# A decoder step with mixture of experts: the routing's marking, ranks, weights and tables, and the order of the work around them

## The chip, the cores and the metric

The kernel runs on one core of one Trainium2 chip. The metric is the device time of one launch in microseconds (us); the kernel before has a median of 1256.03 us over 3 runs (1255.35 to 1258.71).

## The reference

One decoder layer over 576 tokens (512 of a prompt, 64 of eight sampled sequences), width 1024: attention and a gated convolution side by side, a layer norm, and then a feed-forward part. Its routing is what the change is about:

```
scores = sigmoid(x2 @ w_router)                       # 64 experts in 8 groups of 8
biased = scores + router_bias
grp_score = sum(top_k(biased by group, 2))            # keep the 4 best groups
eidx = top_k(where(in a kept group, biased, -inf), 6) # 6 experts of each token
gw = scores[eidx]; gw = gw / sum(gw) * 2.5
y = shared_expert(x2) + sum_j gw_j * expert[eidx_j](x2)
ple = sigmoid(h @ w_ple_gate) * (p @ w_ple_proj)      # added before the last norm
```

Each of the 64 experts has three weight matrices of 1 MB. All are read from HBM, whatever the routing says.

## The kernel before, in words

Tokens lie in NT = 5 tiles of 128 (the last has 64). Each engine has its own program, written out by hand; semaphores alone order the engines, and each engine and each DMA queue does its work strictly in the order written. After the first norm this happens:

- TensorE computes router logits, then the shared expert's gate and up products (`shared_half(m, k, cs)`: half m of the columns, k = 0 gate, 1 up; 6 matmuls for each of 8 chunks c). These accumulate in PSUM tensor `proj` for m = 0 and `att` for m = 1, two banks each for gate and up.
- VectorE picks the experts (lines 1900 to 1950): `max` gives the best eight values of a group or token, `max_index` their places; from these it builds one-hot rows `hot` (30 = 5 tiles x 6 choices, 64 wide) and their sum `sel`. It signals `sel_ready`.
- TensorE turns `sel` into the rank of each token at its expert by small bf16 matmuls into `proj` banks 0 and 1 (L1395, L1398). VectorE's `shared_act(0)` must have read these banks first (`hs_ready`). VectorE copies the ranks out (`rank_read`), computes the number of passes of each pair of experts, its running sum in five doubling steps (L2005, L2006), and a code of column and slot for each choice; `pick(dst, per_expert)` reads a value for each of the 30 choices by multiplying with `hot` and summing (L1964, L1967).
- Table m = 0..9: VectorE builds the pieces for three choices in one of two buffers (L2048 to L2055, `tb_ready`), TensorE multiplies them into one bank (`table_products`, L1407, `tb_used`). `weights_of(t)` on VectorE computes the gate weights of one tile of tokens before every second table. When all ten are summed, VectorE reads the bank out and signals `routed`.
- Between tables TensorE works on 20 gate units: unit u = 5 j + t is column block j (of 4) and token tile t of `h @ w_ple_gate` (L1423, 24 matmuls). N_AHEAD = 3 units stand ahead of table 0, one behind each table, the rest of blocks 0 to 2 behind those. The last block's units (15 to 19) run split in `last_block(True)`, the first transposes of gathered rows (`turn(0)`), and `last_block(False)`.
- A unit goes on through ScalarE (`gate_sigmoid(u)`, L999) and GpSimd (`ple_product(u)`). Unit u on TensorE waits for the sigmoid of unit u - 2. Each column block is loaded as float32 by SyncE (`load_gate(j)`, L587), copied by ScalarE (`gate_hi(j)`, L973), and its low part computed by GpSimd in four instructions (`gate_lo(j)`, L713). Blocks 0 to 3 use two slots, 1, 0, 1, 0. On ScalarE `gate_hi(2)` stands behind the sigmoid of unit 5 and `gate_hi(3)` behind that of unit 11, ahead of that of unit 12. GpSimd does `gate_lo(3)` behind `ple_product(11)`, and then the first gather of rows, which waits for `routed`.
- Expert weights stream through a ring of three buffers, each for a pair of experts, six parts of 1 MB (`load_part`, L595). Pair 0 is loaded when the shared products are done (`su_ready` 2). The first half of pair 1's buffer is where the routing's tables lie, its second half where gate products `ppo` and the shared activations `hs_f` lie. So parts 0 to 2 of pair 1 wait for `routed`, the others for `ppo_added` (VectorE has added units 0 to 9) and `hs_hd` (ScalarE has copied `hs_f` away, behind the sigmoid of unit 14). Pair 2's parts wait for `tb_used` 11 (the end of `last_block(True)`), for all 20 units, and for `res_done`. From pair 3 on each buffer's reload waits for the compute of the pair three before, which runs at TensorE's lines 1493 and 1512.

Of the kernel before, what the change touches and what calls it, by code (L numbers as in the profile page):

```python
# [16 lines left out]
P = 128  # L17
# [38 lines left out]
N_AHEAD = 3  # L56
# [64 lines left out]
def decoder_step(nc, x_prompt, x_sample, p_prompt, p_sample, win_k, win_v, conv_state, w_in, sinks,  # L121
# [4 lines left out]
    with ctx:  # L126
        base0 = (nc.sbuf_base + 31) // 32 * 32

        def at(name, shape, dt, off):
            return nc.alloc_sbuf_tensor_at(name, shape, dt, offset=base0 + off)  # L130
# [141 lines left out]
        hs_f = at("hs_f", [P, 2, T], F32, o_w1 + 38912)  # L272
# [21 lines left out]
        wpick = at("wpick", [P, TOPK, NE], F32, o_w1 + 43520)  # L294
# [18 lines left out]
        ghot = rsm("ghot", [P, NT, TOPG, NGRP], F32)  # L313
# [3 lines left out]
        gidx = rsm("gidx", [P, NT, 8], U32)  # L317
        gidx_f = rsm("gidx_f", [P, NT, TOPG], F32)
# [17 lines left out]
        cums = [rsm(f"cums{i}", [P, NPE], F32) for i in range(2)]  # L336
# [5 lines left out]
        hot_a = at("hot_a", [P, NT, TOPK // 2, NE], BF16, o_w1 + 4096)  # L342
        hot_b = at("hot_b", [P, NT, NE], BF16, o_w1 + 4096 + 2 * NT * TOPK // 2 * NE)
# [148 lines left out]
        def _(sp):  # L492
# [565 lines left out]
        def _(pe):  # L1058
# [329 lines left out]
            shared_half(1, 0, range(KC))  # L1388
            shared_half(1, 1, range(2))

            pe.wait_ge(sel_ready, 1)
            pe.wait_ge(hs_ready, 1)
            for t in range(NT):
                for s in range(t + 1):
                    nc.tensor.matmul(proj[:, 0, t * NE:(t + 1) * NE], (ones_b if s < t else tri_b)[:, :], sel[:, s, :],  # L1395
                                     start=(s == 0), stop=(s == t))
            for s in range(NT):
                last = nc.tensor.matmul(proj[:, 1, 0:NE], ones_b[:, :], sel[:, s, :], start=(s == 0), stop=(s == NT - 1))  # L1398
            last.then_inc(rank_ready, 1)
            shared_half(1, 1, range(2, KC)).then_inc(su_ready, 1)  # L1400
# [188 lines left out]
        def _(dve):  # L1589
# [307 lines left out]
            nc.vector.memset(scores[NS:P, NT - 1, :], 0.0)  # L1897
            dve.wait_ge(sc_ready, 1)
# [13 lines left out]
            for t in range(NT):  # L1912
                nc.vector.max_index(gidx[:, t, :], gbest[:, t, :], gsum[:, t, :])
            dve.drain()

            nc.vector.tensor_copy(gidx_f[:, :, :], gidx[:, :, 0:TOPG])
            dve.drain()
            for t in range(NT):
                nc.vector.tensor_tensor(ghot[:, t, :, :], iota64[:, 0:NGRP].unsqueeze(1).to_broadcast([P, TOPG, NGRP]),
                                        gidx_f[:, t, :].unsqueeze(2).to_broadcast([P, TOPG, NGRP]), ALU.is_equal)  # L1920
            dve.drain()
            nc.vector.reduce_sum(gmask[:, :, :], ghot[:, :, :, :].rearrange("p t i g -> p t g i"), AX.X)
            dve.drain()
            nc.vector.tensor_scalar(gmask[:, :, :], gmask[:, :, :], BIG, -BIG, ALU.mult, ALU.add)
# [8 lines left out]
            dve.drain()  # L1933
            for t in range(NT):
                nc.vector.max_index(eidx[:, t, :], ebest[:, t, :], biased[:, t, :])
# [8 lines left out]
            dve.drain()  # L1944
            hot5 = hot[:, :, :].rearrange("p (t j) e -> p t j e", t=NT)
            nc.vector.tensor_tensor(hot_a[:, :, :, :], hot5[:, :, 0:TOPK // 2, :], hot5[:, :, TOPK // 2:TOPK, :], ALU.add)
            dve.drain()
            nc.vector.tensor_tensor(hot_b[:, :, :], hot_a[:, :, 0, :], hot_a[:, :, 1, :], ALU.add)
            dve.drain()
            nc.vector.tensor_tensor(sel[:, :, :], hot_b[:, :, :], hot_a[:, :, 2, :], ALU.add).then_inc(sel_ready, 1)  # L1950
# [19 lines left out]
            def weights_of(t):  # L1970

                js = slice(t * TOPK, (t + 1) * TOPK)
                total = ssum[:, t:t + 1]
                nc.vector.tensor_tensor(wpick[:, :, :], hot[:, js, :], scores[:, t, :].unsqueeze(1).to_broadcast([P, TOPK, NE]),
                                        ALU.mult)
                dve.drain()
                nc.vector.reduce_sum(wj[:, js], wpick[:, :, :], AX.X)
                dve.drain()
                nc.vector.reduce_sum(total, wj[:, js], AX.X)
                dve.drain()  # L1980
                if t == NT - 1:
                    nc.vector.memset(ssum[NS:P, t:t + 1], 1.0)
                    dve.drain()
                nc.vector.reciprocal(total, total)
                dve.drain()
                nc.vector.tensor_scalar(wj[:, js], wj[:, js], total, ROUTED_SCALE, ALU.mult, ALU.mult)
                dve.drain()

            shared_act(0)
            dve.wait_ge(rank_ready, 1)  # L1990
            nc.vector.tensor_copy(base64[:, :], proj[:, 1, 0:NE:2])
            dve.drain()
            nc.vector.tensor_tensor(nmax[:, :], base64[:, :], proj[:, 1, 1:NE:2], ALU.max)
            dve.drain()
            nc.vector.tensor_scalar(npass_i[:, :], nmax[:, :], SLOT - 1.0, None, ALU.add)
            nc.vector.tensor_copy(rank_i[:, :, :].rearrange("p t e -> p (t e)"), proj[:, 0, 0:NT * NE]).then_inc(rank_read, 1)
            dve.drain()
            nc.vector.tensor_scalar(npass_i[:, :], npass_i[:, :], 6, None, ALU.arith_shift_right)
# [3 lines left out]
            cur = npass_f  # L2002
            for s in range(5):
                nxt = cums[s % 2]
                nc.vector.tensor_copy(nxt[:, 0:1 << s], cur[:, 0:1 << s])  # L2005
                nc.vector.tensor_tensor(nxt[:, 1 << s:], cur[:, 1 << s:], cur[:, 0:NPE - (1 << s)], ALU.add)  # L2006
                dve.drain()
                cur = nxt

            nc.vector.tensor_tensor(base64[:, :], cur[:, :], npass_f[:, :], ALU.subtract)  # L2010

# [24 lines left out]
            nc.vector.tensor_copy(slot_j[:, :], code_j[:, :].bitcast(I32))  # L2036
            dve.drain()
# [208 lines left out]
```

## Time and profile before

| | |
|---|---|
| median of 3 runs | 1256.03 us |
| the profiled execution | 1255.99 us |
| its span | 1254.2 us |
| TensorE matmul busy | 1219.1 us (97%) |
| VectorE / ScalarE / GpSimd busy | 512.2 / 314.7 / 159.3 us |
| DMA | 307.31 MB, mean 245 GB/s |

The span runs from the first to the last recorded instruction; 1.8 us of the execution lie around it. In 40 slices of 31.4 us each the page shows the DMA engines mostly at two to three tenths until about slice 20 (the end of the routing), and at nine tenths from slice 22 on to the end, at about 420 GB/s: there the expert weights stream. The granted clock is at full speed in all slices.

### The profile page before, as it was taken

To read this page: it belongs to the slowest core of one execution; us is meant where nothing else is said; L and a number is where in the kernel's file an instruction comes from. 1 tells how busy PE (TensorE), PEld (TensorE's weight loads), DVE (VectorE), ACT (ScalarE), POOL (GpSimd) and SP (SyncE) were. 2 spreads that over 40 slices of the span, in tenths; PEclk is the share of its full clock that TensorE was granted. 3 is DMA by queue.
4 is the path that set the end of the run, shared out by engine and by line. 5 is a ranking of instruction groups with operands and counts; after the bars stand their busy time and mean duration, and the time that the engine had idled before them with its cause. 6 is when DMAs were issued, how large, how long until landed. Compare 5 with 4: busy or idle time off the path is not lost.

```text
span 1254.2 us, 23439 instructions
## 1 busy us (share of the span) xinstructions
PE 1219.1 (97%) x8816; PEld 982.2 (78%) x8817; DVE 512.2 (41%) x1125; ACT 314.7 (25%) x574; POOL 159.3 (13%) x227
## 2 busy tenths in 40 slices
PE   8999989999999999999899999999999999999987
PEld 8999979999999999998899665556555566666643
DVE  4666783432444324566885112121222221111137
ACT  4364553222212222316012111111111111111121
POOL 0200000000000000004235211111121121212100
PEclk9999999999999999999999999999999999999999
DMA  8222223223232232615428999999999999999987
GB/s 265 80 60 68 68 52 68 68 70 99 68 100 69 77 110 67 213 23 208 175 94 330 420 419 420 420 420 419 420 422 418 420 422 418 419 423 420 421 352 297
DMA packets 98656, 307.31 MB, mean 245 GB/s; under 512 B 11244, under 2 KB 62404, under 8 KB 72840
## 3 DMA queue, kind: packets, MB, share of 16 engines
q1 hardware_dynamic: 85332, 275.20, 56.6%
q0 software_dynamic: 12304, 28.60, 5.9%
q10 hardware_dynamic: 948, 2.50, 0.5%
q8 instruction: 52, 0.85, 0.3%
q14 instruction: 20, 0.16, 0.0%
HBM read 294.45 MB, written 26.94 MB: 256 GB/s over the span
## 4 chain that ended last, share of the span: by engine, by line
PE 56%; DMA 37%; DVE 5%; issue 1%; DVEq 1%; SPq 0%; ACT 0%; ACTq 0%; POOLq 0%
PE proj L1072 32%; DMA w_exp<-in_w_e_down_dram 28%; DMA w_exp<-in_w_e_up_dram 7%; PE proj L1282 4%; PE proj L1423 3%; PE att L1493 3%; PE proj L1512 2%; PE att L1204 1%; PE att L1166 1%; PE att L1291 1%; PE proj L1106 1%; DMA fold<-expert_rows 1%; PE proj L1377 1%; PE proj L1407 1%; PE att L1217 1%
## 5 line engine op out<-in xcount | busy, mean ns | idle before, releaser
L1493 PE MATMUL att<-w_exp,xt 128*64 128x256 f32 x2560 | 286.2, 380 | 1.9 <-DMA w_exp<-in_w_e_up_dram 1.9
L1493 PEld LDWEIGHTS att<-w_exp,xt 128*64 128x64 f32 x2560 | 207.7, 137 | 89.0 <-issue 26.1
L1072 PE MATMUL proj<-h_hi,w_hi 128*128 128x288 f32 x768 | 167.9, 300 | 0.3 <-DVE w_lo L474 0.3
L1072 PE MATMUL proj<-h_hi,w_lo 128*128 128x288 f32 x768 | 164.0, 295 | 0.0
L1072 PE MATMUL proj<-h_lo,w_hi 128*128 128x288 f32 x768 | 163.9, 295 | 0.0
L1512 PE MATMUL proj<-w_exp,ht_e 128*64 128x512 f32 x640 | 146.2, 597 | 9.1 <-issue 5.6
L1072 PEld LDWEIGHTS proj<-h_hi,w_hi 128*128 128x128 f32 x768 | 122.3, 189 | 6.1 <-issue 4.6
L1072 PEld LDWEIGHTS proj<-h_lo,w_hi 128*128 128x128 f32 x768 | 123.6, 188 | 0.0
L1072 PEld LDWEIGHTS proj<-h_hi,w_lo 128*128 128x128 f32 x768 | 123.4, 188 | 0.0
L474 DVE TENSOR_TENSOR w_lo<-w_raw,w_hi 128x2048 fp32r<-128x2048 f32 x33 | 75.6, 2291 | 92.1 <-ACT w_hi L464 87.7
L1512 PEld LDWEIGHTS proj<-w_exp,ht_e 128*64 128x64 f32 x640 | 50.5, 136 | 77.1 <-issue 74.3
L2126 DVE TENSOR_SCALAR ysb<-proj,tabw 128x512 f32 x40 | 30.0, 751 | 139.1 <-PE proj L1512 139.1
L464 ACT ACTIVATE w_hi<-w_raw 128x2048 fp32r<-128x2048 f32 x33 | 63.0, 1910 | 84.5 <-PE proj L1072 73.9
L2117 DVE TENSOR_TENSOR sg<-sg,att 128x256 f32<-128x256 f32 x40 | 16.9, 422 | 117.1 <-ACT sg L1025 117.1
L1032 ACT ACTIVATE ysb<-proj,tabw 128x512 f32 x40 | 27.5, 687 | 140.5 <-PE proj L1512 140.5
L2121 DVE TENSOR_TENSOR h_e<-sg,att 128x256 f32<-128x256 f32 x40 | 16.9, 421 | 111.4 <-PE att L1493 111.4
L693 POOL DMA_DIRECT2D out_dram<-cn_tok x1 | 0.5, 502 | 474.9 <-ACT cn_tok L938 474.9
L1027 ACT ACTIVATE ht_e<-att 128x256 f32<-128x256 f32 x40 | 15.3, 383 | 170.9 <-PE att L1499 170.9
L768 POOL DMA_INDIRECT expert_rows<-ysb,sidx_col x39 | 39.5, 1012 | 131.8 <-DVE ysb L2126 131.8
L1433 PEld LDWEIGHTS proj<-ident,xg 128*128 128x128 f32 x328 | 43.3, 195 | 15.9 <-issue 13.9
L1072 PE MATMUL proj<-mix_hi,w_hi 128*128 128x288 f32 x256 | 54.8, 296 | 0.0
L1072 PE MATMUL proj<-mix_hi,w_lo 128*128 128x288 f32 x256 | 54.8, 296 | 0.0
(392 smaller groups left out, 1864.0 us busy)
## 6 DMA issues: line engine op xcount, KB each, us to landing
w_exp<-in_w_e_gate_dram SPq DMA_DIRECT2D x64, 1024.0 KB
w_exp<-in_w_e_up_dram SPq DMA_DIRECT2D x64, 1024.0 KB
w_exp<-in_w_e_down_dram SPq DMA_DIRECT2D x64, 1024.0 KB
w_raw<-in_w_in_dram SPq DMA_DIRECT2D x21, 1024.0 KB
part<-expert_rows SPq DMA_DIRECT2D x8, 1536.0 KB, 20.4
w_raw<-in_w_in_dram SPq DMA_DIRECT2D x8, 512.0 KB
w_raw<-in_w_attn_out_dram SPq DMA_DIRECT2D x8, 512.0 KB
w_raw<-in_w_conv_out_dram SPq DMA_DIRECT2D x4, 1024.0 KB
```

Of the source, the lines that this page charges most:

```text
L464: nc.scalar.activation(w_hi[:, g.par, :], w_raw[:, g.par, :], ACT.Copy).then_inc(hi_done, 1)
L474: nc.vector.tensor_tensor(w_lo[:, g.par, :], w_raw[:, g.par, :], w_hi[:, g.par, :].bitcast(F32), ALU.subtract).then_inc(w_ready, 1)
L768: pool.indirect_dma_start(out=rows_d[:, :], out_offset=bass.IndirectOffsetOnAxis(ap=sidx_col[i][:, 0:1], axis=0), in_=ysb[:, i, :], in_off ...
L1032: nc.scalar.activation(ysb[:, bass.ds(side_of, 1), 0:512].rearrange("p o n -> p (o n)"), proj[:, 2, :], ACT.Copy, scale=tabw[:, bass.ds(k, ...
L1072: last = nc.tensor.matmul(proj[:, 2 * i + a, 0:HALF], lhs, x[:, c, a * HALF:(a + 1) * HALF], start=(c == 0 and n == 0), stop=(c == KC - 1 ...
L1282: last = nc.tensor.matmul(out, x, v, start=(c == 0 and n == 0), stop=(c == KC - 1 and n == last_term))
L1423: last = nc.tensor.matmul(gate_bank(u)[0:w, :], x[:, c, t * P:t * P + w], v[:, c, :], start=(c == 0 and n == 0), stop=(c == KC - 1 and n = ...
L1433: last = nc.tensor.transpose(proj[:, half, c * P:(c + 1) * P], xg[:, :, half * 4 + c], ident[:, :])
L1493: last = nc.tensor.matmul(att[e * SLOT:(e + 1) * SLOT, m, 0:FF], xt[:, c, e * SLOT:(e + 1) * SLOT], weights[e][:, c, :], start=(c == 0), s ...
L1512: last = nc.tensor.matmul(proj[e * SLOT:(e + 1) * SLOT, 2 + half, :], ht_e[:, c, e * SLOT:(e + 1) * SLOT], down[e][:, c, half * 512:(half ...
L2117: nc.vector.tensor_tensor(sg[:, :], sg[:, :], att[:, 0, 0:FF], ALU.mult)
L2126: nc.vector.tensor_scalar(ysb[:, bass.ds(side_of, 1), 512:D].rearrange("p o n -> p (o n)"), proj[:, 3, :], tabw[:, bass.ds(k, 1)], None, A ...
```

## The change

Routing: groups and experts that are not in the top are no longer found through indices. `gbest`'s last four values are overwritten, `match_replace` marks the kept group scores with BIG, and a mask is made by comparing; likewise `ebest` and `replaced` give `sel`, and `sel_ready` comes before `max_index` and `hot`. The three additions that made `sel` are gone. Ranks go to bank 2 of `att`, ahead of most of `shared_half(1, 0)`; `shared_half(1, 1)`, which uses that bank, waits for `rank_read`. VectorE reads ranks ahead of `shared_act(0)`. One `tensor_tensor_scan` replaces the doubling steps; the code of column and slot takes fewer passes. The weights of all tiles are computed at once, before table 0. `shared_act(1)` stands before table 4 instead of table 2. TensorE does four units ahead of the tables, and then units behind tables 1, 3, 5, 7, 8 and 9. SyncE loads parts 0 to 2 of pair 1 ahead of gate block 3, and part 4 with part 3.

```
-N_AHEAD = 3
+N_AHEAD = 4
+UNIT_AFTER = (1, 3, 5, 7, 8, 9)
-        hs_f = at("hs_f", [P, 2, T], F32, o_w1 + 38912)
+        hs_f = at("hs_f", [P, 2, T], F32, o_w1 + 49152 - 2 * 4 * T)
+        def rank_out(t):
+            return att[:, 2, t * NE:(t + 1) * NE]
@@ SyncE
             load_gate(2)
+            sp.wait_ge(routed, 1)
+            load_parts(1, 1, range(3))
             sp.wait_ge(u_ready, 2 * NT)
             load_gate(3)
-            sp.wait_ge(routed, 1)
-            load_parts(1, 1, range(3))
             sp.wait_ge(ppo_added, 1)
-            load_parts(1, 1, range(3, 4))
+            load_parts(1, 1, range(3, 5))
             sp.wait_ge(hs_hd, 1)
-            load_parts(1, 1, range(4, 6))
+            load_parts(1, 1, range(5, 6))
@@ TensorE
-            shared_half(1, 0, range(KC))
-            shared_half(1, 1, range(2))
-
+            shared_half(1, 0, range(2))
             pe.wait_ge(sel_ready, 1)
-            pe.wait_ge(hs_ready, 1)
...
             last.then_inc(rank_ready, 1)
-            shared_half(1, 1, range(2, KC)).then_inc(su_ready, 1)
+            shared_half(1, 0, range(2, KC))
+            pe.wait_ge(rank_read, 1)
+            shared_half(1, 1, range(KC)).then_inc(su_ready, 1)
+            pe.wait_ge(hs_ready, 1)
             for u in range(N_AHEAD):
                 gate_unit(u)
-            pe.wait_ge(rank_read, 1)
             for m in range(NTK // TPAIR):
                 table_products(m)
-                gate_unit(N_AHEAD + m)
-            for u in range(N_AHEAD + NTK // TPAIR, 3 * NT):
+                if m in UNIT_AFTER:
+                    gate_unit(N_AHEAD + UNIT_AFTER.index(m))
+            for u in range(N_AHEAD + len(UNIT_AFTER), 3 * NT):
                 gate_unit(u)
@@ VectorE (max_index, gidx_f, ghot and the sum over ghot are gone)
+            nc.vector.memset(gbest[:, :, TOPG:8], 4 * BIG)
...
+                nc.vector.match_replace(gmask[:, t, :], gbest[:, t, :], gsum[:, t, :], BIG)
+            nc.vector.tensor_scalar(gmask[:, :, :], gmask[:, :, :], BIG, -BIG, ALU.not_equal, ALU.mult)
...
+            nc.vector.memset(ebest[:, :, TOPK:8], 4 * BIG)
...
+                nc.vector.match_replace(replaced[:, t, :], ebest[:, t, :], biased[:, t, :], BIG)
+            nc.vector.memset(replaced[NS:P, NT - 1, :], 0.0)
+            nc.vector.tensor_scalar(sel[:, :, :], replaced[:, :, :], BIG, None, ALU.is_equal).then_inc(sel_ready, 1)
...
-            nc.vector.tensor_tensor(hot_a[:, :, :, :], hot5[:, :, 0:TOPK // 2, :], hot5[:, :, TOPK // 2:TOPK, :], ALU.add)
-            nc.vector.tensor_tensor(hot_b[:, :, :], hot_a[:, :, 0, :], hot_a[:, :, 1, :], ALU.add)
-            nc.vector.tensor_tensor(sel[:, :, :], hot_b[:, :, :], hot_a[:, :, 2, :], ALU.add).then_inc(sel_ready, 1)
...
+            nc.vector.tensor_tensor_scan(cums[:, :], npass_f[:, :], no_steps[:, :], 0.0, ALU.add, ALU.add)
+            nc.vector.tensor_tensor(base64[:, :], cur[:, :], npass_f[:, :], ALU.subtract)
+            nc.vector.scalar_tensor_tensor(slot_map[:, :, :], col_i, float(P), slot_map[:, :, :].bitcast(I32), ALU.mult, ALU.add)
             for t in range(NT):
+                nc.vector.scalar_tensor_tensor(col_map[:, t, :].rearrange("p (q e) -> p q e", e=2),
+                                               base64[:, :].unsqueeze(2).to_broadcast([P, NPE, 2]), float(P),
+                                               slot_map[:, t, :].rearrange("p (q e) -> p q e", e=2), ALU.mult, ALU.add)
...
+            pick(wj[:, :], scores)
+            wj3 = wj[:, :].rearrange("p (t j) -> p t j", t=NT)
+            nc.vector.reduce_sum(ssum[:, :], wj3, AX.X)
+            nc.vector.memset(ssum[NS:P, NT - 1:NT], 1.0)
+            nc.vector.reciprocal(ssum[:, :], ssum[:, :])
+            nc.vector.scalar_tensor_tensor(wj3, wj3, ROUTED_SCALE, ssum[:, :].unsqueeze(2).to_broadcast([P, NT, TOPK]),
+                                           ALU.mult, ALU.mult)
             for m in range(NTK // TPAIR):
-                if m == 2:
+                if m == 4:
                     shared_act(1)
-                if m % 2 == 0:
-                    weights_of(m // 2)
```

## Rows read from the trace of the kernel before

**Rows 1.** The page, part 4: the chain that ended last, by engine.

```profile
...
PE 56%; DMA 37%; DVE 5%; issue 1%; DVEq 1%; SPq 0%; ACT 0%; ACTq 0%; POOLq 0%
```

**Rows 2.** Chain of waits, 480 to 700 us: start, length, what ran.

```profile
...
599.09 8.00 PE att L1377 x60
...
624.59 2.14 PE proj L1407 x6
626.73 3.42 PE proj L1423 x24
630.15 0.92 PE proj L1407 x6
631.07 2.74 PE proj L1423 x24
...
661.14 8.48 PE proj L1423 x72
669.62 5.76 PE att L1447 x48
...
679.12 0.88 PE proj L1433 x8
```

**Rows 3.** Who waited for whom, 560 to 700 us: total, times, longest.

```profile
...
PE proj L1407 <- DVE tab_b L2055: 3.4, 1, 3.4
...
DVE base L1991 <- PE proj L1398: 1.2, 1, 1.2
```

**Rows 4.** Windows: length, busy PE, PEld, DVE, ACT, POOL, then PEclk, DMA share, GB/s.

```profile
...
172.00:174.00 2.00, 0.53 (x5) 0.29 (x3) 1.83 (x8) 0.11 (x1) 0.00 (x0) 1.00 0.00 0
603.55:605.07 1.52, 1.52 (x14) 1.52 (x13) 1.33 (x4) 0.00 (x0) 0.00 (x0) 1.00 0.00 0
609.40:611.05 1.65, 1.65 (x14) 1.65 (x13) 1.28 (x10) 0.00 (x0) 0.00 (x0) 1.00 0.00 0
614.00:618.75 4.75, 4.75 (x42) 4.75 (x42) 4.58 (x6) 0.77 (x2) 1.15 (x1) 1.00 0.91 378
624.00:626.00 2.00, 1.41 (x5) 1.44 (x6) 1.85 (x5) 0.00 (x0) 0.00 (x0) 0.60 1.03 434
628.00:630.00 2.00, 2.00 (x19) 2.00 (x19) 1.63 (x6) 0.00 (x0) 0.00 (x0) 1.00 0.55 225
678.00:680.00 2.00, 2.00 (x20) 2.00 (x19) 0.00 (x0) 0.00 (x0) 0.00 (x0) 1.00 0.98 332
```

**Rows 5.** SyncE in order of time: start, length, DMAs issued.

```profile
...
612.58 0.82 SPq L595 DMA_DIRECT2D w_exp<-in_w_e_gate_dram  x2
...
633.84 19.23 SPq L587 DMA_DIRECT2D pg_raw<-in_w_ple_gate_dram  x2
662.66 0.82 SPq L595 DMA_DIRECT2D w_exp<-in_w_e_gate_dram  x2
...
679.15 1.42 SPq L595 DMA_DIRECT2D w_exp<-in_w_e_gate_dram  x2
```

**Rows 6.** The tile pg_raw: conversion of a gate block, and loads to landing.

```profile
...
L973 ACT ACTIVATE pg_hi<-pg_raw x4: 1898/1907/1916, 588.1 to 660.5; 128x2048 fp32r<-128x2048 f32 x4
...
DMA to landing us min/median/max: 5.1/5.2/9.2
```

**Rows 7.** GpSimd in order of time: two conversions of a gate block.

```profile
...
640.97 5.21 POOL L713 TENSOR_TENSOR pg_lo<-pg_raw,pg_hi 128x512 fp32r<-128x512 f32 x4 [2.15 <-ACT pg_hi L973]
...
662.53 5.60 POOL L713 TENSOR_TENSOR pg_lo<-pg_raw,pg_hi 128x512 fp32r<-128x512 f32 x4 [1.06 <-ACT pg_hi L973]
```

**Rows 8.** VectorE in order of time: a search of the selection, table building.

```profile
...
600.64 0.22 DVE L1935 FIND_INDEX8 eidx<-ebest,biased 128x8 uint32<-128x64 f32 x1
...
622.51 0.44 DVE L2048 TENSOR_TENSOR tab_b<-cc,col_j 128x270 f32<-128x270 f32 x1
...
624.36 0.43 DVE L2048 TENSOR_TENSOR tab_b<-cc,col_j 128x270 f32<-128x270 f32 x1
...
643.60 1.45 DVE L2048 TENSOR_TENSOR tab_b<-cc,col_j 128x270 f32<-128x270 f32 x1
```

More of the change, by code:

```diff
@@ L293, in decoder_step @@
         NTK = NT * TOPK
-        wpick = at("wpick", [P, TOPK, NE], F32, o_w1 + 43520)
         picked = at("picked", [P, NTK, NE], F32, o_w1 + 4096)
@@ L312, in decoder_step @@
         best8 = rsm("best8", [P, NT * NGRP, 8], F32)
-        ghot = rsm("ghot", [P, NT, TOPG, NGRP], F32)
+        replaced = at("replaced", [P, NT, NE], F32, o_w1 + 4096)
         sel = rsm("sel", [P, NT, NE], BF16)
@@ L316, in decoder_step @@
         gbest = rsm("gbest", [P, NT, 8], F32)
-        gidx = rsm("gidx", [P, NT, 8], U32)
-        gidx_f = rsm("gidx_f", [P, NT, TOPG], F32)
         gmask = rsm("gmask", [P, NT, NGRP], F32)
@@ L335, in decoder_step @@
         npass_f = rsm("npass_f", [P, NPE], F32)
-        cums = [rsm(f"cums{i}", [P, NPE], F32) for i in range(2)]
+        cums = rsm("cums", [P, NPE], F32)
         slot_j, col_j, code_j = (rsm(n, [P, NTK], F32) for n in ("slot_j", "col_j", "code_j"))
@@ L341, in decoder_step @@
         hot = rsm("hot", [P, NTK, NE], BF16)
-        hot_a = at("hot_a", [P, NT, TOPK // 2, NE], BF16, o_w1 + 4096)
-        hot_b = at("hot_b", [P, NT, NE], BF16, o_w1 + 4096 + 2 * NT * TOPK // 2 * NE)
+        no_steps = rsm("no_steps", [P, NPE], F32)
         assert next_routing[0] <= o_w1 + 28672
@@ L1387, in _ @@
             pe.wait_ge(sc_ready, 1)
-            shared_half(1, 0, range(KC))
-            shared_half(1, 1, range(2))
+            shared_half(1, 0, range(2))
             pe.wait_ge(sel_ready, 1)
-            pe.wait_ge(hs_ready, 1)
             for t in range(NT):
[L1394 to L1398, printed above, removed]
+                for k in range(t + 1):
+                    nc.tensor.matmul(rank_out(t), (ones_b if k < t else tri_b)[:, :], sel[:, k, :],
+                                     start=(k == 0), stop=(k == t))
+            for k in range(NT):
+                last = nc.tensor.matmul(rank_out(NT), ones_b[:, :], sel[:, k, :], start=(k == 0), stop=(k == NT - 1))
             last.then_inc(rank_ready, 1)
-            shared_half(1, 1, range(2, KC)).then_inc(su_ready, 1)
+            shared_half(1, 0, range(2, KC))
+            pe.wait_ge(rank_read, 1)
+            shared_half(1, 1, range(KC)).then_inc(su_ready, 1)
             def table_products(m):
@@ L1897, in _ @@
             nc.vector.memset(scores[NS:P, NT - 1, :], 0.0)
+            nc.vector.memset(no_steps[:, :], 0.0)
             dve.wait_ge(sc_ready, 1)
@@ L1911, in _ @@
             dve.drain()
[L1912 to L1916, printed above, removed]
+            nc.vector.memset(gbest[:, :, TOPG:8], 4 * BIG)
             dve.drain()
             for t in range(NT):
-                nc.vector.tensor_tensor(ghot[:, t, :, :], iota64[:, 0:NGRP].unsqueeze(1).to_broadcast([P, TOPG, NGRP]),
-                                        gidx_f[:, t, :].unsqueeze(2).to_broadcast([P, TOPG, NGRP]), ALU.is_equal)
+                nc.vector.match_replace(gmask[:, t, :], gbest[:, t, :], gsum[:, t, :], BIG)
             dve.drain()
-            nc.vector.reduce_sum(gmask[:, :, :], ghot[:, :, :, :].rearrange("p t i g -> p t g i"), AX.X)
-            dve.drain()
-            nc.vector.tensor_scalar(gmask[:, :, :], gmask[:, :, :], BIG, -BIG, ALU.mult, ALU.add)
+            nc.vector.tensor_scalar(gmask[:, :, :], gmask[:, :, :], BIG, -BIG, ALU.not_equal, ALU.mult)
             dve.drain()
@@ L1933, in _ @@
             dve.drain()
+            nc.vector.memset(ebest[:, :, TOPK:8], 4 * BIG)
+            dve.drain()
+            for t in range(NT):
+                nc.vector.match_replace(replaced[:, t, :], ebest[:, t, :], biased[:, t, :], BIG)
+            dve.drain()
+            nc.vector.memset(replaced[NS:P, NT - 1, :], 0.0)
+            dve.drain()
+            nc.vector.tensor_scalar(sel[:, :, :], replaced[:, :, :], BIG, None, ALU.is_equal).then_inc(sel_ready, 1)
             for t in range(NT):
@@ L1943, in _ @@
                                     ALU.is_equal)
-            dve.drain()
-            hot5 = hot[:, :, :].rearrange("p (t j) e -> p t j e", t=NT)
-            nc.vector.tensor_tensor(hot_a[:, :, :, :], hot5[:, :, 0:TOPK // 2, :], hot5[:, :, TOPK // 2:TOPK, :], ALU.add)
-            dve.drain()
-            nc.vector.tensor_tensor(hot_b[:, :, :], hot_a[:, :, 0, :], hot_a[:, :, 1, :], ALU.add)
-            dve.drain()
-            nc.vector.tensor_tensor(sel[:, :, :], hot_b[:, :, :], hot_a[:, :, 2, :], ALU.add).then_inc(sel_ready, 1)
             def shared_act(m):
@@ L1968, in pick @@
                 dve.drain()
[L1970 to L1989, printed above, removed]
             dve.wait_ge(rank_ready, 1)
-            nc.vector.tensor_copy(base64[:, :], proj[:, 1, 0:NE:2])
+            nc.vector.tensor_copy(base64[:, :], rank_out(NT)[:, 0:NE:2])
             dve.drain()
-            nc.vector.tensor_tensor(nmax[:, :], base64[:, :], proj[:, 1, 1:NE:2], ALU.max)
+            nc.vector.tensor_tensor(nmax[:, :], base64[:, :], rank_out(NT)[:, 1:NE:2], ALU.max)
             dve.drain()
             nc.vector.tensor_scalar(npass_i[:, :], nmax[:, :], SLOT - 1.0, None, ALU.add)
-            nc.vector.tensor_copy(rank_i[:, :, :].rearrange("p t e -> p (t e)"), proj[:, 0, 0:NT * NE]).then_inc(rank_read, 1)
+            nc.vector.tensor_copy(rank_i[:, :, :].rearrange("p t e -> p (t e)"), att[:, 2, 0:NT * NE]).then_inc(rank_read, 1)
             dve.drain()
+            shared_act(0)
             nc.vector.tensor_scalar(npass_i[:, :], npass_i[:, :], 6, None, ALU.arith_shift_right)
@@ L2001, in _ @@
             dve.drain()
[L2002 to L2010, printed above, removed]
+            nc.vector.tensor_tensor_scan(cums[:, :], npass_f[:, :], no_steps[:, :], 0.0, ALU.add, ALU.add)
+            cur = cums
             col_i = col_map[:, :, :].bitcast(I32)
@@ L2036, in _ @@
             nc.vector.tensor_copy(slot_j[:, :], code_j[:, :].bitcast(I32))
+            pick(wj[:, :], scores)
+            wj3 = wj[:, :].rearrange("p (t j) -> p t j", t=NT)
+            nc.vector.reduce_sum(ssum[:, :], wj3, AX.X)
+            dve.drain()
+            nc.vector.memset(ssum[NS:P, NT - 1:NT], 1.0)
+            dve.drain()
+            nc.vector.reciprocal(ssum[:, :], ssum[:, :])
+            dve.drain()
+            nc.vector.scalar_tensor_tensor(wj3, wj3, ROUTED_SCALE, ssum[:, :].unsqueeze(2).to_broadcast([P, NT, TOPK]),
+                                           ALU.mult, ALU.mult)
             dve.drain()
             for m in range(NTK // TPAIR):
-                if m == 2:
+                if m == 4:
                     shared_act(1)
-                if m % 2 == 0:
-                    weights_of(m // 2)
                 js, r = slice(m * TPAIR, (m + 1) * TPAIR), m % 2
```

7 lines of the change are left out of this document (removed).

## The prediction

> **What bounds the kernel now.** I read the chain of waits first: 56% of it is TensorE, 37% is DMA [rows 1]. The change touches nothing ahead of about 590 us, so the question is how its stretch hands over to the rest. The chain in order of time [rows 2] shows TensorE unbroken from the shared products (599.09) on, then one hole in front of the first table (624.59), then tables and gate units back to back to 669.62, the last block of units, and turn(0) at 679.12. Behind that the chain is mostly DMA: the expert weights stream.
>
> So I ask when that stream starts. SyncE issues pair 2's first parts at 679.15 [rows 5], when the first pass over the last block has ended. In the window 678 to 680 the DMA has just run low, 332 instead of about 424 GB/s [rows 4]: pair 1 had landed just then. So a shift of TensorE's 679.12 mark shifts the whole stream, and with it the end, one for one. Loading pair 1 earlier adds nothing by itself, since pair 2 may not be issued before that mark. Everything below prices the shift of this mark.
>
> **The selection and ranks.** Gone are three additions in front of `sel` and the index work on groups; new are 10 match-and-replace steps (priced like the 0.22 us search [rows 8], which they resemble), memsets and a compare. `sel` was ready at 605.1, the end of the three additions (1.5 us) [rows 4]. These and the one-hot pass with its searches (about 3.7) no longer stand ahead of it, the group indices save about 1.5, the marking of experts adds about 1.5: `sel` is ready at about 600, give or take 1. TensorE now asks for it after a quarter of shared_half(1, 0), at about 600.5, so the two meet. But TensorE did not wait for it before either: the 60 matmuls run 8.00 us without a break [rows 2]. The 20 rank matmuls only change their place. Gain on TensorE 0; a late `sel` costs 0 to 0.5 us; I take 0. The new wait for `rank_read` has behind it the second half of the shared products; rank reading should end about 604.6, TensorE arrives 4.8 us after the ranks (six chunks of 0.8 us, 8.00/10), at 606. Cost 0.
>
> **The hole before the tables.** TensorE stands idle for 3.4 us until VectorE has built table 0 [rows 3]. The hole costs more than its length: the granted clock falls to 0.60 in the window after it [rows 4], that is, part of it runs at the lower level (1.2 GHz) instead of 2.4, and table 0 takes 2.14 us against 0.92 of a later one, and the unit behind it 3.42 against 2.87 (8.48 us for the last three, one of which is the short tile's 2.74) [rows 2]. That is 1.2 + 0.55 = 1.8 us, so 5.2 us hang on the hole.
> After the change, TensorE comes out of the ahead units later: they began at 624.59 - 3.4 - 3 x 2.87 = 612.6 and four of them last until 624.1. VectorE's side: table 0 was ready at about 624.5. Taken off: the 1.2 us wait for ranks [rows 3], the three additions (1.5), the doubling steps for one scan (the window 609.40 to 611.05, 1.65, less 0.35 for one small instruction, 1.3), and two casts and a pass of the code (0.65, one and a half such instructions of 0.44 [rows 8]). Added: a full pick of the weights (4.7, the window 614.00 to 618.75 [rows 4], a pick from end to end) and about 1.0 for its tail, less the 2.4 that one tile's weights took (a pick of a fifth the size and its tail): 3.3. So 624.5 - 4.6 + 3.3 = 623.2, 0.9 ahead of TensorE. The hole is gone: the fourth unit, moved from behind it, fills it. If that cover fails, each us costs one, and the 1.8 on top from somewhere below 3.4.
> If nothing else waits, ten tables (9.2) and five units (4 x 2.87 + 2.74 = 14.2) follow: table 9 ends at 624.1 + 23.4 = E = 647.5.
>
> **The tables in pairs.** VectorE needs 1.85 us for one (622.51 to 624.36 [rows 8]) and may be only two ahead. A pair of tables and a unit are 4.7 us on TensorE, two builds 3.7, so it keeps pace by 1.0. Two things eat that. shared_act(1), 1.5 us, stands before table 4. And gate_lo(2) on GpSimd, 5.21 us in four instructions [rows 7], slows VectorE's builds: at 643.60 the first instruction of one takes 1.45 instead of 0.44 [rows 8]. Today VectorE is two tables ahead and hides it. After the change unit 4 ends at about 629, gate block 2 is issued then and lands 5.2 us later [rows 6], its copy takes 1.9 [rows 6], so gate_lo(2) runs from 636.2 to 641.3, with the build of table 7 inside. Four instructions at 1.0 us extra, less what overlaps: 3.5. That build ends at 641.8 where TensorE wants table 7 at 639.3, a stall of about 2.6, and 0.3 more falls at table 1. Bounds: 0, if the two do not meet, and 5.2 (all of gate_lo). I take 2.9, from the row of the slow build: E = 650.4 (647.5 to 652.7).
> The Trainium skill, SBUF — State Buffer, section Who interferes with whom, has VectorE instructions with two SBUF inputs and GpSimd instructions that read SBUF block each other for a whole instruction. By that rule four builds' instructions could lose all four of GpSimd's, 5.2 us, and E would be 652.7; the 643.60 row agrees with blocking, at 1.0 us for one.
>
> `routed` comes 1.5 us after E, so near 652 instead of 662.66 [rows 5]. This looks like a gain of 10 us, but TensorE only did the tables first; the units it skipped come after.
>
> **What is late next: gate block 3.** Behind E stand units 9 to 14: 4 x 2.87 + 2 x 2.74 = 17.0 us. Alone, that would put the last block's start at 667.4 (E = 650.4) against 669.62. But that block needs gate_lo(3), and unit 14 needs the sigmoid of unit 12, which stands behind gate_hi(3) on ScalarE. Gate 3's slot comes free with unit 9, E + 2.8, as 3 MB of expert weights have just entered the same queue at E + 1.5. Today it is issued alone (at about 652.7, the second load of the row at 633.84 [rows 5]) and lands in 5.2 us. Pair 0's six parts took from 612.58 plus 1.7 us of start to about 629.1 (the window at 628 is half full [rows 4]), 2.47 us each. So gate 3 lands at E + 1.5 + 1.7 + 3 x 2.47 + 3.5 = E + 14.1 instead of E + 8. That loads can hold up a later one is seen in the maximum, 9.2 us [rows 6]. Then the copy, to E + 16.0; unit 14 starts at E + 16.3 instead of E + 14.2; gate_lo(3), 5.05 to 5.6, ends at E + 21.3. Bounds: landing at E + 8 (not held up, nothing lost) and E + 15.
> The last block therefore starts at E + 21.3 = 671.7, 2.1 us later than 669.62 [rows 2]. From there 9.5 us to the mark, as now. TensorE's two idle spells, 2.1 and 2.2 us, lie between a hole of 1.5 us that left the clock at 1.00 (window at 172) and the one of 3.4 that did not [rows 4, 3]; bounds 0 to 1.8 us, I take 0.
> The gather behind gate_lo(3), part 5 (issued near E + 26 behind the sigmoid of unit 14) and part 4's earlier release have 7 us or more of slack before their use; cost 0. The new DMA gap before part 5 does not count, as pair 2 is held by the mark.
>
> **Sum.** Hole and clock -5.2, ahead unit and pairing are neutral in work, stalls in the tables +2.9, gate 3's lateness +4.2 (E + 21.3 against E + 17.0), and 0.2 of rounding: +2.1 us. The profiled execution took 1255.99, 0.04 below the median, so I predict 1256.0 + 2.1 = 1258.1 us, with 1255.5 to 1260 as this case's own range. 0.3%, or 3.8 us, is what a measurement of this kernel can tell from no change.
>
> **Rivals.**
> (A) Gate 3 is not held up: it lands by E + 8 since its requests share the engines with the parts. Then the last block starts at E + 17.0, and the mark moves by -2.2 (E = 650.4) to -5.1 (E = 647.5): 1253.8 to 1250.9 us. For it: the routing itself is short work of VectorE and the hole does go. Against: one queue, and the 9.2 us landing.
> (B) Slower: the two idle spells before the last block drop the clock. They do so if they count as long, somewhere between 1.5 and 3.4 us each. Then the last block pays the 1.8 us that the hole cost: 1258.1 + 1.8 = 1259.9, and with E at its upper bound, 652.7, 1262.2.
> (C) The mark does not hold the stream: parts loaded from 652 on instead of 662.66 count by themselves, less the 2.5 us of gate 3 now inside. Then the gain is 10.7 - 2.5 = 8.2: 1247.8 us. Against it speaks the dip at 678.
>
> **Chances.** My forecast 0.48 (of it 0.08 above 1259.8), A 0.25 (0.14 below 1252.2), B 0.18, C 0.09. So faster 0.23, same 0.51, slower 0.26. Leaving out C and B's far end gives 1250.9 to 1261.5.
>
> **What would show it.** Right: no idle before table 0 and a clock of 1.00 there; a wait of 2 to 3 us at a table near 640; gate 3 landing 11 us after its issue; a wait of ScalarE's pg_hi for that DMA, and of TensorE's L1423 and L1447 behind it; turn(0) at 681. Wrong: gate 3 landing in 5 us and the last block starting at once; `sel` or the first table late; or a stream that is ahead of turn(0).

## The result, and the profile after

The changed kernel takes 1264.21 us (median of 5 runs, 1261.52 to 1266.52), the kernel before 1257.0 (5 runs, 1255.35 to 1259.57). The ratio is 1.0053 (95% interval 1.004 to 1.0066): about 6.7 us slower (the medians differ by 7.2). Forecast was 1258.1 within 1250.9 to 1261.5: the measured time lies above it. The profiled execution took 1264.15 us, against 1255.99 before, 8.2 more.

The chain of waits of the changed kernel, where it answers to [rows 2] (start, length, what ran):

```profile
...
627.27 1.18 PE proj L1407 x6
...
644.79 2.17 PE proj L1407 x6
646.96 3.23 PE proj L1423 x24
...
657.72 13.33 DMA pg_raw<-in_w_ple_gate_dram
...
673.30 5.32 PE proj L1423 x24
678.62 5.75 PE att L1447 x48
...
688.12 0.88 PE proj L1433 x8
```

Three things stand out. Table 7 starts at 644.79 and takes 2.17 us, and the unit behind it 3.23. The chain then leaves TensorE at the end of table 9 (654.9), and from 657.72 on it is one load, gate block 3, of 13.33 us. And unit 14, which follows its conversion, takes 5.32 us instead of 2.74 before the last block starts at 678.62. turn(0), the mark, is at 688.12 instead of 679.12: 9.0 us late.

Who waited for whom in the changed kernel, the rows that answer to [rows 3] (total, times, longest):

```profile
...
ACT pg_hi L974 <- DMA pg_raw<-in_w_ple_gate_dram: 7.6, 2, 7.3
...
PE proj L1407 <- DVE tab_b L2030: 4.3, 2, 3.3
PE proj L1423 <- ACT sig_g L1000: 4.2, 1, 4.2
...
PE att L1393 <- DVE sel L1936: 0.8, 1, 0.8
```

The hole of 3.4 us in front of table 0 is gone, but with nothing to spare: VectorE has table 0 ready at 624.99, and TensorE comes to it at 625.04. In its place TensorE waits 0.8 us for `sel`, 4.3 us at two tables (1.0 at table 1, 3.3 at table 7), and 4.2 us in front of unit 14 for a sigmoid, which itself is behind the 7.3 us wait of pg_hi for the DMA.

Windows of the changed kernel, as [rows 4] (length, busy PE, PEld, DVE, ACT, POOL, PEclk, DMA share, GB/s):

```profile
...
644.00:646.00 2.00, 1.21 (x4) 1.21 (x5) 2.00 (x3) 0.00 (x0) 1.32 (x2) 0.57 0.03 8
...
670.00:675.00 5.00, 1.70 (x8) 1.70 (x9) 0.00 (x0) 2.46 (x3) 1.95 (x2) 0.66 0.68 281
675.00:680.00 5.00, 5.00 (x31) 5.00 (x30) 0.00 (x0) 0.00 (x0) 4.05 (x5) 0.66 0.01 3
```

The clock is at 0.57 behind the hole at table 7, and at 0.66 around unit 14: in part of each window it is at 1.2 GHz.

SyncE's issues, as [rows 5], and the landing row of the tile pg_raw, as [rows 6]:

```profile
...
656.40 0.80 SPq L596 DMA_DIRECT2D w_exp<-in_w_e_gate_dram  x2
657.24 0.43 SPq L596 DMA_DIRECT2D w_exp<-in_w_e_up_dram  x1
657.72 0.64 SPq L588 DMA_DIRECT2D pg_raw<-in_w_ple_gate_dram  x1
```

```profile
...
DMA to landing us min/median/max: 5.2/7.1/13.3
```

`routed` is indeed 6.3 us earlier (656.40 for 662.66), and gate 3 is issued 1.3 us behind the parts and lands in 13.3 us.

VectorE building table 7, and GpSimd beside it, as [rows 8] and [rows 7]:

```profile
...
638.82 1.53 DVE L2023 TENSOR_TENSOR tab_b<-cc,col_j 128x270 f32<-128x270 f32 x1
640.27 1.62 DVE L2025 TENSOR_TENSOR tab_a<-cc,slot_j 128x384 f32<-128x384 f32 x1
641.97 1.34 DVE L2028 TENSOR_TENSOR tab_b<-tab_b,cc 128x270 f32<-128x270 f32 x1
643.39 1.34 DVE L2030 TENSOR_TENSOR tab_b<-tab_b,wj 128x270 f32<-128x270 f32 x1
```

```profile
...
638.61 5.83 POOL L714 TENSOR_TENSOR pg_lo<-pg_raw,pg_hi 128x512 fp32r<-128x512 f32 x4 [1.50 <-ACT pg_hi L974]
```

The four instructions of this table take 1.3 to 1.6 us each while gate_lo(2) runs from 638.61 to 644.44; for the table before it they take 0.44 to 0.56.

### The profile page after: what moved, and what is told of

Its sections match the earlier page's. It is cut to its first block, busy times and chain, and to the rows that moved or that the text cites. A ratio compares the mean times of both kernels' runs of the same rounds, so it can differ in the third digit from the quotient of the medians.

```text
span 1262.3 us, 23387 instructions
## 1 busy us (share of the span) xinstructions
PE 1223.2 (97%) x8816; PEld 984.3 (78%) x8817; DVE 502.1 (40%) x1103; ACT 314.8 (25%) x574; POOL 158.1 (13%) x227
## 4 chain that ended last, share of the span: by engine, by line
PE 57%; DMA 33%; DVE 7%; issue 1%; DVEq 1%; ACT 0%; SPq 0%; ACTq 0%; POOLq 0%
PE proj L1073 31%; DMA w_exp<-in_w_e_down_dram 29%; PE att L1494 5%; PE proj L1283 4%; PE proj L1513 3%; PE proj L1423 1%; PE att L1205 1%; PE att L1167 1%; PE att L1292 1%; DMA pg_raw<-in_w_ple_gate_dram 1%; PE proj L1107 1%; DMA fold<-expert_rows 1%; PE proj L1433 1%; PE att L1218 1%; PE att L1447 1%
## 5 line engine op out<-in xcount | busy, mean ns | idle before, releaser
L1073 PE MATMUL proj<-mix_lo,w_hi 128*128 128x288 f32 x256 | 54.8, 296 | 0.0
```

The lines of the kernel that those rows point to most:

```text
L1073: last = nc.tensor.matmul(proj[:, 2 * i + a, 0:HALF], lhs, x[:, c, a * HALF:(a + 1) * HALF], start=(c == 0 and n == 0), stop=(c == KC - 1 ...
```

## The experiments

In the order below the kernels are called g3_first, b_g3_behind, g3_lo2cut, g3_lo2late, a_lo2late, g3_single, g3_first_extra and g3_single_extra, routing_only, a_gate_alone and best. Each is compared with the kernel before by a ratio of runs on the same chip. For the profiled executions two times are used: the mark (start of turn(0) in the chain of waits) and the issue of pair 1's first part.

### Gate block 3 ahead of the parts

```
+            sp.wait_ge(u_ready, 2 * NT)
+            load_gate(3)
             sp.wait_ge(routed, 1)
             load_parts(1, 1, range(3))
-            sp.wait_ge(u_ready, 2 * NT)
-            load_gate(3)
```

> The changed kernel with one thing undone: SyncE loads gate block 3 ahead of parts 0 to 2 of pair 1, as before. Theory Q (the three parts in the queue make gate 3 late, and TensorE's last block waits for its low part): gate 3, issued at about 657.7, lands in about 5.2 us instead of 13.3; unit 14 follows unit 13 without a wait; the last block starts at about 671.9 instead of 678.6, turn(0) at 681.4 instead of 688.1, and the time falls by 6.7 us to about 1257.5. Rival S (the expert stream decides, gate 3 is hidden behind it): the wait goes, but the parts land later by the 2.5 us of gate 3, and the time stays at 1264 or rises by up to 2.

1257.75 us (12 runs, 1252.45 to 1260.59), ratio 1.0005 (0.9996 to 1.0014): the slowdown is gone, and theory Q stands. Its chain, in the execution that was profiled (1252.45 us, the shortest of the twelve and 5.3 us below their median):

```profile
...
641.20 1.18 PE proj L1407 x6
...
649.95 16.99 PE proj L1423 x144
666.94 5.76 PE att L1447 x48
...
676.44 0.88 PE proj L1433 x8
```

Units 9 to 14 run in one piece of 16.99 us, and the last block starts where they end. The hole at table 7 was 2.2 us in this execution:

```profile
...
PE proj L1407 <- DVE tab_b L2030: 2.2, 1, 2.2
```

```profile
...
640.00:642.00 2.00, 0.80 (x5) 0.81 (x6) 2.00 (x2) 0.00 (x0) 2.00 (x2) 1.00 0.00 0
642.00:644.00 2.00, 2.00 (x18) 2.00 (x17) 1.93 (x3) 0.00 (x0) 1.16 (x2) 1.00 0.03 8
```

The clock stays at 1.00 and table 7 takes 1.18 us. More than this hole was short in this execution. The compare that makes `sel` took 0.59 us while gate_lo(1) ran on GpSimd, where the ten other profiled kernels with this compare show 1.39 to 1.40:

```profile
...
597.99 0.59 DVE L1936 TENSOR_SCALAR sel<-replaced 128x320 bf16<-128x320 f32 x1
```

Two instructions ahead of it took 0.63 and 0.49 us instead of 1.53 and 1.48, and TensorE waited neither for `sel` nor at table 1. In another kernel with the same order of tables (g3_first_extra, below) these three instructions took 1.54, 1.48 and 1.40 us, the hole at table 7 was 3.8 us, the table took 2.17, the mark came at 681.69 (theory Q had 681.4), and the time was 1257.3. Of the 5.2 us between the two marks 2.3 arise ahead of the hole, 1.6 in it and 1.3 behind it, at the lowered clock. So it varies from execution to execution how long GpSimd's conversions hold VectorE up. That is the likeliest reason for the spread of 8 us, but only the profiled executions show it.

### The same swap alone, in the kernel before

The same lines in the order of the changed kernel, nothing else.

> The kernel before with this one thing done alone: gate block 3 behind parts 0 to 2 of pair 1. Theory Q: gate 3 can't be issued before routed (662.7) and lands some 13 us later, near 677; its copy ends at 679, its low part at 684; the last block starts there instead of at 669.6, with up to 2 us more for a lowered clock: 14 to 16 us slower than before, 1271 to 1273. Rival S: the time is set by the stream, which starts at the same routed: 1257 to 1259.

1271.79 us, ratio 1.0117 (1.0102 to 1.0133), as theory Q had it. Its chain of waits:

```profile
...
661.08 16.91 issue
...
678.03 4.99 POOL pg_lo L713 x4
...
683.15 5.98 PE att L1447 x48
...
692.88 0.88 PE proj L1433 x8
```

The last block waits for gate_lo(3) until 683.15. This order of the loads alone costs 14 us there, more than in the changed kernel. The likeliest reason is the work left to cover it: behind table 9 TensorE has units 12 to 14 there (8.5 us), and units 9 to 14 in the changed kernel (17.0 us).

### No reading by GpSimd in gate_lo(2)

```
+                    if j == 2:
+                        last = nc.gpsimd.memset(pg_lo[i][:, cols].bitcast(F32), 0.0)
+                        continue
```

> As g3_first, but GpSimd writes zeros instead of computing the low part of gate block 2, so four instructions that read SBUF become four that only write (the low-part product of that block is left out of the result). Theory P: VectorE's instructions of table 7 take 0.44 to 0.55 us instead of 1.3 to 1.6, the wait of 3.3 us at table 7 and the lowered clock (1.6 us) go, table 9 ends near 650, and the time is 4 to 5 us below g3_first, near 1252.5. Rival V (VectorE is simply too slow for two tables in a row, whatever GpSimd does): a wait of 2 to 3 us at table 7 stays, and the gain is under 1.5 us.

1251.97 us (1251.81 to 1252.57), ratio 0.9956 (0.9942 to 0.9969), 5.8 us below g3_first. Table 7's instructions on VectorE, and GpSimd beside them:

```profile
...
638.66 0.43 DVE L2026 TENSOR_TENSOR tab_b<-cc,col_j 128x270 f32<-128x270 f32 x1
639.01 0.55 DVE L2028 TENSOR_TENSOR tab_a<-cc,slot_j 128x384 f32<-128x384 f32 x1
...
640.16 0.44 DVE L2033 TENSOR_TENSOR tab_b<-tab_b,wj 128x270 f32<-128x270 f32 x1
```

```profile
...
638.23 1.92 POOL L715 MEMSET pg_lo<- 128x512 f32 x4 [1.28 <-ACT pg_hi L977]
```

The table's first three instructions fall within GpSimd's four, which only write (638.23 to 640.15), and take 0.43 to 0.55 us; the fourth starts as these end. Theory P stands. These instructions were also shorter (1.92 us together, not 5.8), so that part alone doesn't part reading from being busy.

### gate_lo(2) behind unit 7, all work done

```
-                if u in (NT, 2 * NT + 1):
+                if u in (NT + 2, 2 * NT + 1):
                     gate_lo(u // NT + 1)
```

> As g3_first, all work done, but GpSimd computes the low part of gate block 2 behind the product of unit 7 instead of unit 5, when VectorE has nearly built its last table. Theory P (VectorE's builds are blocked by GpSimd's four instructions): no wait at table 7, table 9 ends near 650, and since unit 10 starts near 652.7 and the low part is done near 651.5, the time is that of g3_lo2cut, 1252 to 1253. Rival L (the low part is late for unit 10 in its new place): a wait in front of unit 10 takes the place of the one at table 7, and the time is 1255 to 1258.

1252.46 us (1251.93 to 1253.36), ratio 0.9957 (0.9944 to 0.9971): faster than both kernels with nothing left out. Its chain:

```profile
...
642.02 1.83 PE proj L1407 x12
643.86 2.87 PE proj L1423 x24
...
651.43 16.99 PE proj L1423 x144
...
677.92 0.88 PE proj L1433 x8
```

Tables 6 and 7 run as one piece of 1.83 us, and the units behind table 9 in one piece.

The same edit in the changed kernel, with gate 3 still late:

> The changed kernel with gate 3 still behind the parts, and only the low part of gate 2 moved behind unit 7. Theory P with additive terms: table 9 ends 4.5 to 5 us earlier, and everything behind it, gate 3's issue and late landing too, moves with it: 1259 to 1260. Rival A (gate 3's lateness covers the wait at table 7): 1263 to 1264.

1259.97 us, ratio 1.0022 (1.0014 to 1.0031). Between the profiled executions gate 3's issue moves from 657.72 to 653.77 and the mark from 688.12 to 684.28, 3.9 each. The terms add up; the lateness doesn't cover the hole.

### One unit behind every table

```
-UNIT_AFTER = (1, 3, 5, 7, 8, 9)
+UNIT_AFTER = tuple(range(10))       # with gate 3 ahead of the parts
```

> As g3_first, and in addition one unit behind every table again instead of tables in pairs (four units stay ahead). Theory P (the pairing takes away the time in which VectorE builds; GpSimd's low part of gate 2 then shows as a stall at table 7 and as a lowered clock behind it): no wait at tables 1 and 7; table 9 ends at about 660 instead of 655, but turn(0) comes at 675 to 676, 4 us earlier than in the kernel before, and the time is 1253 to 1255. Rival R (an early routed is worth more than TensorE's waits, as the first parts of pair 1 load sooner): routed is 5 us later than in g3_first, so it is slower than g3_first.

1257.3 us, ratio 0.9996 (0.9987 to 1.0005): a miss. The waits at the tables are gone and the mark is early, as expected:

```profile
...
661.10 5.60 PE proj L1423 x48
...
676.21 0.90 PE proj L1433 x8
```

```profile
...
664.12 0.82 SPq L596 DMA_DIRECT2D w_exp<-in_w_e_gate_dram  x2
```

```profile
...
670.00:675.00 5.00, 5.00 (x44) 5.00 (x43) 1.75 (x6) 0.00 (x0) 1.44 (x2) 1.00 1.03 420
675.00:680.00 5.00, 5.00 (x45) 5.00 (x44) 0.69 (x1) 1.36 (x3) 1.92 (x3) 1.00 1.00 395
```

But `routed` comes at 664, and the DMA engines are full from there on without a gap (420 and 395 GB/s). The time is that of the kernel before, with a mark 2.9 us earlier and `routed` 1.5 us later. So the prediction's rule, that the mark alone sets the end, fails here: an earlier mark gave nothing.

### 1 MB more behind routed

```
-            load_parts(1, 1, range(3))
+            sp.dma_start(w_exp[1][:, 0, 0, :], ...).then_inc(ld_cv, 16)   # part 0, once more
+            load_parts(1, 1, range(1, 3))
+            sp.wait_ge(ld_cv, 32)
+            load_parts(1, 1, range(1))
```

> As g3_first, with 1 MB more to load: part 0 of pair 1 is loaded twice. Theory M (here the stream starts with the mark, the end of the first pass over the last block, and the DMA engines have some 2.5 us of idle before it): the time stays within 0.7 us of g3_first. Rival N (every byte behind routed counts): 2.5 us slower than g3_first.

> As g3_single, with the same 1 MB more. There routed comes 8 us later than in the best execution of g3_first, the mark at the same 676.2, and no idle of the DMA engines is left between them. Theory M says that such a kernel is bound by the bytes behind routed: 2.5 us slower than g3_single. If the mark alone decides, as the prediction had it: no change.

Ratios 1.0009 (1.0 to 1.0018) against 1.0005, and 1.0006 (0.9997 to 1.0015) against 0.9996: 0.5 and 1.3 us more. The order is that of theory M, but 1.3 us is half of the 2.5 it asked for, and the intervals overlap; the medians decide nothing. The profiled executions show more:

| kernel | time | mark | time - mark | issue of pair 1 | time - issue |
|---|---|---|---|---|---|
| changed | 1264.15 | 688.12 | 576.0 | 656.40 | 607.8 |
| a_lo2late | 1260.24 | 684.28 | 576.0 | 652.45 | 607.8 |
| g3_first | 1252.45 | 676.44 | 576.0 | 653.21 | 599.2 |
| g3_first_extra | 1257.3 | 681.69 | 575.6 | 658.39 | 598.9 |
| g3_lo2cut | 1252.57 | 676.33 | 576.2 | 653.09 | 599.5 |
| g3_lo2late | 1253.36 | 677.92 | 575.4 | 654.69 | 598.7 |
| before | 1255.99 | 679.12 | 576.9 | 662.66 | 593.3 |
| routing_only | 1252.16 | 675.05 | 577.1 | 658.58 | 593.6 |
| g3_single | 1257.35 | 676.21 | 581.1 | 664.12 | 593.2 |
| b_g3_behind | 1270.0 | 692.88 | 577.1 | 662.28 | 607.7 |
| best | 1253.49 | 676.20 | 577.3 | 656.63 | 596.9 |

The first six have gaps in the DMA behind `routed`, and their time is the mark + 575.4 to 576.2. The next three issue pair 1 late, and their time is that issue + 593.2 to 593.6. g3_single, 5 us beyond its mark, can't be explained by the mark. g3_single_extra, 1258.1 us with its issue at 663.03, is at 595.1: 1.8 us more for the extra MB.

For the kernel before, two readings are left. One is that the later of the two ends decides and that both meet there. But the last two rows (b_g3_behind, and best, the last experiment) fit neither end: they have gaps in the DMA, and lie at 577.1 and 577.3 behind their marks. They share one thing with the kernel before (576.9) and with routing_only (577.1): parts 4 and 5 of pair 1 go together, 5.3 to 6.0 us ahead of the mark, and bytes still move when pair 2 is issued. In the us behind the mark these four move 205 to 270 GB/s and the first six 12 to 78, as here before and after:

```profile
...
679.12:680.12 1.00, 1.00 (x12) 1.00 (x11) 0.08 (x1) 0.08 (x1) 0.04 (x1) 1.00 0.83 246
...
688.12:689.12 1.00, 1.00 (x11) 1.00 (x11) 0.08 (x1) 0.08 (x1) 0.05 (x1) 1.00 0.11 29
```

So the us between 576 and 577 may come from these two late parts and not from `routed`. No run changes them alone; that stays open.

### The routing's edits without the new order

In the kernel before: marking, ranks in bank 2 of `att`, scan, shorter code. `weights_of(t)`, three units ahead, one unit behind each table and gate 3 ahead of the parts stay, as do shared_act(1) before table 2 and part 4 of pair 1 going with part 5.

> The kernel before with the routing's part of the change alone: marking, ranks in their own bank ahead of most of the shared products, one scan, the shorter code. The gate weights are still computed a tile at a time, three units stand ahead, one unit behind each table, gate block 3 ahead of pair 1. Theory W (computing all weights ahead of table 0 ate what the other edits of the routing gained): table 0 is built near 622 instead of 624.5; the hole in front of it is under 1 us instead of 3.4, with no lowered clock; routed near 658 and turn(0) near 674; 4 to 5 us faster than before, near 1253. Rival Z (VectorE's chain ahead of table 0 is bound elsewhere, by the blocked one-hot pass): table 0 near 624 and the time within 1 us of before.

1252.98 us (1252.16 to 1254.49), ratio 0.9967 (0.9955 to 0.9979). Table 0 on VectorE:

```profile
...
619.66 0.96 DVE L2042 TENSOR_TENSOR tab_b<-tab_b,wj 128x270 f32<-128x270 f32 x1
```

It is ready at 620.6 instead of 624.5, so no hole is left; in the changed kernel it is ready at 625.0. The weights that stand ahead of table 0 take VectorE 2.0 us here (from 616.1) and 6.0 in the changed kernel (from 616.4). Theory W stands: computing all weights first gave back the 4 us that the other edits had won.

### Parts 3 and 4 behind gate 3's landing

```
             sp.wait_ge(ppo_added, 1)
+            sp.wait_ge(pw_in[0], 32)
             load_parts(1, 1, range(3, 5))
```

> The changed kernel; SyncE issues parts 3 and 4 of pair 1 only when gate block 3 has landed, so that these two, issued 3 and 5 us behind gate 3, can't share the engines with it. Theory G (loads issued later take engine time from one that is under way): gate 3 lands 11 us after its issue instead of 13.3, the mark comes 2 us earlier, near 686, and the time is about 1262. Rival F (the queue is served strictly in order, and the 13.3 us have another reason): landing, mark and time as in the changed kernel, 1264.

1264.7 us, ratio 1.0054 (1.0041 to 1.0068): no change. Theory G falls. The tile pg_raw and three windows (as above):

```profile
...
DMA to landing us min/median/max: 5.2/7.1/12.9
```

```profile
...
670.00:671.00 1.00, 1.00 (x11) 1.00 (x9) 0.00 (x0) 0.00 (x0) 0.00 (x0) 1.00 0.54 170
671.00:672.00 1.00, 0.27 (x3) 0.07 (x1) 0.00 (x0) 0.00 (x0) 0.00 (x0) 1.00 0.07 24
672.00:673.00 1.00, 0.00 (x0) 0.00 (x0) 0.00 (x0) 0.21 (x1) 0.00 (x0) 1.00 0.02 6
```

Gate 3 lands 12.9 us behind its issue with nothing behind it in the queue. Almost all bytes have moved by 670.6, the landing shows at 672.7: some 2 us of a nearly idle tail, against under 1 us when it is loaded alone. What the tail is stays open.

### An attempt at both ends

```
-UNIT_AFTER = tuple(range(10))       # routing_only
+UNIT_AFTER = (0, 1, 2, 3, 4, 5, 6, 7, 9)
-            shared_half(1, 0, range(2))
+            shared_half(1, 0, range(3))
```

> As routing_only, with TensorE asking for sel after three chunks instead of two, and no unit between tables 8 and 9. From the profiled executions so far, the time is the later of two ends: mark + 576 us, and the issue of pair 1's first part + 593.2 us. For routing_only these are 1251.1 and 1251.8. Moving one unit behind table 9 brings routed 2.9 us earlier (byte end 1249), asking for sel later brings the mark 0.8 us earlier (1250.3): 1250 to 1251.5, 1 to 2.5 us below routing_only. Rival: the byte end isn't real, and only the 0.8 us show.

1253.93 us, ratio 0.9975 (0.9964 to 0.9986): not below routing_only, a miss. Pair 1 was issued at 656.63, 2 us earlier, but the mark came at 676.20 instead of 675.05: TensorE no longer waited for `sel` and waited 1.1 us at two tables instead. The chain through VectorE to the tables was no shorter than in routing_only: asking later for `sel` doesn't make it ready earlier. The later of the two ends would be 1252.2 here (mark + 576), 1.3 us below what was measured, so this execution doesn't bear that rule out.

## Why the prediction was wrong

**Right.** The hole before table 0 goes. The stall moves to table 7, through GpSimd's gate_lo(2). Gate block 3 is late behind three parts, unit 14 waits for a sigmoid behind its copy, and the last block for its low part. The mark decides for this kernel (time - mark 576.0). g3_first and b_g3_behind show the late load by undoing it and by doing it alone, g3_lo2cut and g3_lo2late the block by gate_lo(2). The direction, slower, was the forecast's, but its 2.1 us lay within what can't be told from no change, and the measured 6.7 us did not.

That the hole before table 0 went was in part luck. I had table 0 ready 0.9 us ahead of TensorE; it was ready at 625.0, 1.8 us later than my 623.2, and only because `sel` held TensorE up as well did the two meet without a hole.

**The step that failed: "I take 2.9 ... E = 650.4"**, the end of table 9. It was 654.9, above the bound of 652.7. From 647.5 without a stall: 1.1 us for `sel` (0.8 of it the wait; the units ahead start at 613.5 instead of 612.4), 1.0 at table 1 with 0.3 of slower running, 3.3 at table 7, and 1.6 of clock behind it (2.17 for 0.92, 3.23 for 2.87) make 654.8. Of these I had 2.6 at table 7 and 0.3 at table 1. Two of the misses were choices:
- The clock. I charged 1.8 us for the old hole, and nothing for a new one of nearly the same length. Where the hole was 2.2 us, the clock stayed at 1.00 (g3_first); at 3.3 it fell to 0.57. That is 1.6 us, and my upper bound on E left it out too.
- `sel`. I put it at 600, "give or take 1", and took 0. It was ready at 601.6. The compare that makes it took 1.40 us, which no term of mine had:

```profile
...
600.19 1.40 DVE L1936 TENSOR_SCALAR sel<-replaced 128x320 bf16<-128x320 f32 x1
```

It started while gate_lo(1) ran on GpSimd. In the kernel before, a scalar operation on 40 elements at 596.22 takes 1.13 us beside the same conversion, so the price was to be had. The Trainium skill, SBUF — State Buffer, section Who interferes with whom, counts `tensor_scalar` among the operations that can contend with GpSimd, not only those with two SBUF inputs, for which I had quoted it. The 1.40 us agree, but g3_first's 0.59 us beside the same conversion show that the price is not paid every time. No run here shows this compare without GpSimd beside it.

**The second size: gate 3's lateness, "+4.2 (E + 21.3 against E + 17.0)".** The last block began at E + 23.7, +6.7. Landing was E + 16.1, not E + 14.1, beyond my bound of E + 15. The queue in order explains 14.5 of it (issue at E + 2.8, bytes done 10.8 later in a_gate_alone, and the 0.9 us of tail of a load alone); a tail of 2 us was in no row of mine. Another 0.6 came from unit 14 at the lower clock, which ended just behind the low part.

4.5 for E and 2.4 here make the 6.9 us between +2.1 and the mark's +9.0. Of these 9.0 the time shows 8.2: **"one for one" was wrong** too. The end came 576.9 us behind the mark before and 576.0 after. Either `routed` and the bytes behind it held the kernel before as much as the mark did, or the last two parts of pair 1 did it, which move earlier in the changed kernel (the table above); the runs don't part these. A gain of the mark alone can give nothing, as in g3_single. I had seen the dip to 332 GB/s and read it as the mark's doing alone: pair 1 was still landing.

**The rivals.** A (gate 3 not held up) is out: 13.3 us. B (the clock) was right on the mechanism and wrong on the place: it fell at table 7 and at unit 14, not in the last block, which took 9.5 us as ever. C (bytes count) is refuted for this kernel: `routed` came 6.3 us earlier, and the time rose. It holds in g3_single.

## What to carry to other kernels

Before a load is moved ahead in a queue, look who waits for the loads that it now stands ahead of: 3 MB of weights, issued at 656 and not read before 706 (until then TensorE works on pair 0), held up 1 MB on which three engines waited. Where a hole is closed by letting the consumer do other work first, count what the producer does beside a second engine that blocks it, and charge a new hole for the lowered clock as the old one was. And where a stream can be held at two places, compute both: a change that moves one earlier gives only the distance to the other.

## What was not expected of the hardware

- A load of 1 MB behind three others in one queue had moved nearly all its bytes 10.8 us behind its issue and landed at 12.9 (a_gate_alone); alone its tail was under 1 us.
- One VectorE instruction of 320 elements that compares and writes bf16 took 1.40 us beside GpSimd's subtraction in the changed kernel, and 0.59 beside the same subtraction in g3_first.
- `match_replace` on 64 elements took 0.21 us and 0.08 to 0.09 for loading its values, as the search does (the 0.22 us of [rows 8]).
